# Mixing's SSM half by token block: the first block through both column halves, then the second

## The reference, cut to what matters

```python
merged = jnp.concatenate([rms_norm_2(y_ssm, g_ssm_out[l]), rms_norm_2(y_attn, g_attn_out[l])], axis=-1)
h = h + rms_norm_2(merged @ w_out[l], g_post_mix[l])

hn = rms_norm_2(h, g_pre_ffn[l])
gu = hn @ w_gate_up[l]
ff = (jax.nn.silu(gu[..., :D_FF]) * gu[..., D_FF:]) @ w_down[l]
h = h + rms_norm_2(ff, g_post_ffn[l])
```

## Time and profile before

| | |
|---|---|
| median of 3 runs | 795.18 us (792.7 to 795.67) |
| profiled execution, its own time | 792.62 us |
| its span, first to last instruction | 790.8 us |
| TensorE matmul / weight load busy | 775.9 us (98%) / 678.8 us (86%) |
| VectorE, ScalarE, GpSimd busy | 514.8 (65%), 405.1 (51%), 233.1 (29%) |
| mean granted TensorE clock | 0.998 |

### The profile page before, as it was taken

The page is one execution under the profiler, slowest core; times in us unless marked ns, Lnnn a source line. Parts: engine busy times, 40 slices in busy tenths (PEclk is TensorE's granted clock), DMA queues, the critical chain, the costliest instruction groups (busy, mean ns, idle before and its releaser), DMA issues.

```text
span 790.8 us, 12710 instructions
## 1 busy us (share of the span) xinstructions
PE 775.9 (98%) x5139; PEld 678.8 (86%) x5139; DVE 514.8 (65%) x753; ACT 405.1 (51%) x649; POOL 233.1 (29%) x186
## 2 busy tenths in 40 slices
PE   8999999999999999999999999998999999999996
PEld 7889988999889889987778888997887888888885
DVE  4746874764557557865557965776678676777453
ACT  5744446534465535344335545717766555556341
POOL 3031895670742000046009910126002111011010
PEclk9999999999999999999999999999999999999999
DMA  9897995387621554654545555430363656655641
GB/s 231 201 247 210 239 229 129 90 195 172 158 80 55 188 184 134 213 179 142 158 134 159 185 192 183 136 132 2 133 225 117 195 184 214 186 184 164 223 175 54
DMA packets 78110, 130.72 MB, mean 165 GB/s; under 512 B 4447, under 2 KB 28243, under 8 KB 77923
## 3 DMA queue, kind: packets, MB, share of 16 engines
q1 hardware_dynamic: 76608, 124.96, 54.2%
q0 software_dynamic: 1200, 4.83, 1.9%
q10 hardware_dynamic: 242, 0.11, 0.0%
HBM read 128.82 MB, written 1.06 MB: 164 GB/s over the span
## 4 chain that ended last, share of the span: by engine, by line
PE 87%; DVE 4%; DMA 3%; ACT 3%; issue 1%; POOL 0%; DVEq 0%; SPq 0%; POOLq 0%; ACTq 0%
PE ps L1515 13%; PE ps L1519 13%; PE ps L1523 13%; PE ps L1555 10%; PE ps L1534 6%; PE ps L1538 6%; PE ps L1542 6%; PE ps L1559 5%; DMA stage<-in_even_w_in 3%; PE ps L1626 2%; PE ps L1645 2%; DVE w_lo L921 1%; ACT w_hi L634 1%; PE ps L1658 1%; PE ps L1657 1%
## 5 line engine op out<-in xcount | busy, mean ns | idle before, releaser
L921 DVE TENSOR_TENSOR w_lo<-stage,w_hi 128x1024 fp32r<-128x1024 f32 x226 | 297.6, 1337 | 162.7 <-ACT w_hi L634 162.0
L634 ACT ACTIVATE w_hi<-stage 128x1024 fp32r<-128x1024 f32 x232 | 242.2, 1060 | 236.9 <-PE ps L1523 112.3
L1515 PE MATMUL ps<-w_hi,act_t 128*128 128x512 f32 (+1 forms) x376 | 102.7, 395 | 1.5 <-ACT w_hi L634 1.0
L1523 PE MATMUL ps<-w_lo,act_t 128*128 128x512 f32 (+1 forms) x376 | 98.7, 385 | 0.1
L1555 PE MATMUL ps<-act_t,w_hi 128*128 128x512 f32 x352 | 88.3, 393 | 0.7 <-DVE act_t L958 0.7
L1515 PEld LDWEIGHTS ps<-w_hi,act_t 128*128 128x128 f32 x376 | 67.9, 188 | 16.8 <-issue 2.8
L1523 PEld LDWEIGHTS ps<-w_lo,act_t 128*128 128x128 f32 x376 | 69.6, 188 | 14.8 <-DVE w_lo L921 0.6
L1519 PE MATMUL ps<-w_hi,act_t 128*128 128x512 f32 (+1 forms) x312 | 81.6, 384 | 0.0
L1555 PEld LDWEIGHTS ps<-act_t,w_hi 128*128 128x128 f32 x352 | 63.3, 189 | 12.2 <-issue 0.9
L1519 PEld LDWEIGHTS ps<-w_hi,act_t 128*128 128x128 f32 x312 | 57.6, 188 | 12.1 <-issue 0.2
L1534 PE MATMUL ps<-act_t,w_hi 128*128 128x256 f32 x416 | 58.9, 284 | 0.4 <-ACT w_hi L634 0.4
(11 more groups left out here) (364 smaller groups left out, 1197.4 us busy)
## 6 DMA issues: line engine op xcount, KB each, us to landing
stage<-in_even_w_in SPq DMA_DIRECT2D x64, 512.0 KB, 5.5
stage<-in_odd_w_in SPq DMA_DIRECT2D x48, 512.0 KB, 4.1
stage<-in_w_gate_up SPq DMA_DIRECT2D x44, 512.0 KB, 4.5
stage<-in_w_down SPq DMA_DIRECT2D x22, 512.0 KB, 4.4
stage<-in_even_w_out SPq DMA_DIRECT2D x16, 512.0 KB, 4.2
stage<-in_odd_w_out SPq DMA_DIRECT2D x16, 512.0 KB, 3.9
stage<-in_w_in SPq DMA_DIRECT2D x10, 512.0 KB, 3.7
stage<-in_w_out SPq DMA_DIRECT2D x8, 512.0 KB, 5.0
```

The costliest lines, as they stand in the source:

```text
L634: nc.scalar.activation(w_hi[:, u % RING, :], stage[:, u % RING, :], ACT.Copy).then_inc(hi_ready, 1)
L921: nc.vector.tensor_tensor(w_lo[:, u % RING, :], stage[:, u % RING, :], w_hi[:, u % RING, :].bitcast(F32), ALU.subtract).then_inc(lo_ready, 1)
L1515: mm(out[:, b, :], a_hi(k)[:, tok[b]], hi[:, i, :], start=(k == 0), stop=False)
L1523: ins = mm(out[:, b, :], a_hi(k)[:, tok[b]], lo[:, i, :], start=False, stop=(k == k_tiles - 1))
```

## The change

- TensorE: `mix_ssm` runs block 0 through half 0 and half 1, then block 1 through both, twelve matmuls for each pair. All four weight units are released in block 1. Before the last six matmuls (block 1, half 1, second unit) TensorE turns block 0 of x. Behind them it waits for half 0's drain, issues `keep_busy(9)`, waits for all low parts of block 0 (`first_lo`) and turns block 1.
- The turned tiles are split by block, 128 x 128 each (`hi_of_block`, `lo_of_block`), 16 + 16 instructions for 8 + 8. Block 0's stand ahead of block 1's last sum on VectorE, and ahead of its last square on ScalarE.
- `mix_gain` writes its product to another buffer (`ssm_out` for half 0, `gate_z` for half 1), so it waits for the sum alone and no longer for the square. `x_add` reads there.
- The sums go in the order (0,0), (1,0), (0,1), (1,1).
- `take_attn_half(1)` comes ahead of `squares(5)` on ScalarE.
- The splits of weights stand elsewhere. Up to the last unit of `mix_ssm` they are made before mixing's sums, both parts. The high parts of the next two follow block 0's squares. VectorE makes the low parts of the FFN's units between and behind the low parts of block 1 of x.

```diff
 # ScalarE
             hi_of_turned(3 * KD + 20, 4, 4, COL_GSSM)
+            take_attn_half(1)
             squares(5, lambda b: ssm_out[:, b, :], lambda b: gate_z[:, b, :])
-            take_attn_half(1)
-            ahead(("mix_ssm", 0))
...
+            split_hi(last_unit[("mix_ssm", 1)] + 1)
...
+            def hi_of_block(b, made):
+
+                for k in range(KD):
+                    act.wait_ge(x_turned, KD * b + (k | 1) + 1)
+                    o = 4 * BANK + k * S + b * P
+                    nc.scalar.activation(act_t[:, k, b * P:(b + 1) * P], ps[:, o:o + P], ACT.Copy, scale=col[:, COL_FFN + k:COL_FFN + k + 1]).then_inc(made, 1)
+
+            mix_squares(0, 0)
+            mix_squares(1, 0)
+            split_hi(last_unit[("mix_ssm", 1)] + 3)
+            mix_squares(0, 1)
+            hi_of_block(0, first_hi)
+            mix_squares(1, 1)
+            hi_of_block(1, act_hi)
             ahead(("mix_ssm", 1))
-            hi_of_turned(3 * KD + 24, KD, 0, COL_FFN)
             act.wait_ge(x_ready, 2 * NB)
 # VectorE
+            gained = (ssm_out, gate_z)
+
             def mix_gain(c, b):
 
-                dve.wait_ge(squared, squared_count(5) + 2 * c + b + 1)
-                return TT(mixed[:, b, halves[c]], mixed[:, b, halves[c]], row_a[:, halves[c]], ALU.mult)
+                dve.wait_ge(mixed_ready, 2 * b + c + 1)
+                TT(gained[c][:, b, :], mixed[:, b, halves[c]], row_a[:, halves[c]], ALU.mult).then_inc(drain_sem(("mix_ssm", c)) if b == 1 else mix_gained, 1)
...
+            split_lo(last_unit[("mix_ssm", 1)] + 1)
+            for c in range(2):
+                chunk_drained(dve, ("mix_attn", c))
+                dve.wait_ge(mix_block, c + 1)
+                mix_sum(c, 0)
+                mix_gain(c, 0)
+            mix_mean(0)
+            x_add(0, 0)
+            x_add(1, 0)
             chunk_done(dve, ("mix_ssm", 0))
...
+            mix_sum(0, 1)
+            mix_gain(0, 1)
+            lo_of_block(0, range(KD), first_hi, 0, first_lo)
             chunk_done(dve, ("mix_ssm", 1))
             mix_sum(1, 1)
...
+            mix_gain(1, 1)
             mix_mean(1)
...
             x_add(0, 1)
             x_add(1, 1)
-            lo_of_turned(3 * KD + 24, 4, 0, COL_FFN, KD)
-            split_lo(next_unit[0] + 1)
-            lo_of_turned(3 * KD + 28, 4, 4, COL_FFN + 4, KD + 4)
+            lo_of_block(1, range(4), act_hi, 3 * KD + 24, act_lo)
+            split_lo(last_unit[("mix_ssm", 1)] + 2)
+            lo_of_block(1, range(4, 8), act_hi, 3 * KD + 24, act_lo)
             split_lo(last_unit[("ffn", 0)] + 1)
 # TensorE
+            def turn_block(b):
+
+                for k in range(KD):
                     if k % 4 == 0:
                         pe.wait_ge(x_ready, 2 * b + k // 4 + 1)
                     o = 4 * BANK + k * S + b * P
-                    ins = nc.tensor.transpose(ps[:, o:o + P], x[:, b, k * P:(k + 1) * P], ident[:])
-                    if b == 1:
-                        ins.then_inc(turned, 1)
+                    nc.tensor.transpose(ps[:, o:o + P], x[:, b, k * P:(k + 1) * P], ident[:]).then_inc(x_turned, 1)
...
+                        if b == 1:
+                            ins.then_inc(unit_used, 1)
+                        if (b, c, j) == (1, 1, 0):
+                            turn_block(0)
+                    if b == 0:
+                        ins.then_inc(mix_block, 1)
+            chunk_drained(pe, ("mix_ssm", 0))
+            keep_busy(9, number[("mix_ssm", 0)] % 2 * 2)
+            pe.wait_ge(first_lo, KD)
+            turn_block(1)
```

More of the change, by code:

```diff
@@ L260, in build @@
         turned, act_hi, act_lo = sem("turned"), sem("act_hi"), sem("act_lo")
-        x_ready, h_ready, mix_gained = sem("x_ready"), sem("h_ready"), sem("mix_gained")
+        x_ready, x_turned, h_ready, mix_gained, first_hi, first_lo = (sem(n) for n in ("x_ready", "x_turned", "h_ready", "mix_gained", "first_hi", "first_lo"))
         dve_step, act_step, pool_step = sem("dve_step"), sem("act_step"), sem("pool_step")
@@ L867, in _, with mix_squares @@
             hi_of_turned(3 * KD + 20, 4, 4, COL_GSSM)
+            take_attn_half(1)
             squares(5, lambda b: ssm_out[:, b, :], lambda b: gate_z[:, b, :])
-            take_attn_half(1)
-            ahead(("mix_ssm", 0))
[L871 to L875, removed]
+            split_hi(last_unit[("mix_ssm", 1)] + 1)
+            def mix_squares(c, b):
+                act.wait_ge(mixed_ready, 2 * b + c + 1)
+                half = slice(c * 512, (c + 1) * 512)
+                nc.scalar.activation(junk[:, b, half], mixed[:, b, half], ACT.Square, scale=D**-0.5, accum_out=(sumsq, sumsq_b)[c][:, 12 + b:13 + b]).then_inc(squared, 1)
+            def hi_of_block(b, made):
[10 more added lines that the diff above has]
+            hi_of_block(1, act_hi)
             ahead(("mix_ssm", 1))
-            hi_of_turned(3 * KD + 24, KD, 0, COL_FFN)
             act.wait_ge(x_ready, 2 * NB)
@@ L1358, in mix_sum @@
                 STT(mixed[:, b, halves[c]], result(("mix_ssm", c))[:, b, :], rstd[:, 10 + b:11 + b], mixed[:, b, halves[c]], ALU.mult, ALU.add).then_inc(mixed_ready, 1)
+            gained = (ssm_out, gate_z)
             def mix_gain(c, b):
-                dve.wait_ge(squared, squared_count(5) + 2 * c + b + 1)
-                return TT(mixed[:, b, halves[c]], mixed[:, b, halves[c]], row_a[:, halves[c]], ALU.mult)
+                dve.wait_ge(mixed_ready, 2 * b + c + 1)
+                TT(gained[c][:, b, :], mixed[:, b, halves[c]], row_a[:, halves[c]], ALU.mult).then_inc(drain_sem(("mix_ssm", c)) if b == 1 else mix_gained, 1)
             def mix_mean(b):
-                dve.wait_ge(squared, squared_count(5) + 2 + b + 1)
+                dve.wait_ge(squared, squared_count(5) + 2 * b + 2)
                 c = slice(12 + b, 13 + b)
@@ L1373, in x_add @@
                 dve.wait_ge(rstd_ready, 7 + b)
-                STT(x[:, b, halves[c]], mixed[:, b, halves[c]], rstd[:, 12 + b:13 + b], x[:, b, halves[c]], ALU.mult, ALU.add).then_inc(x_ready, 1)
-            ahead(("mix_ssm", 0))
-            chunk_drained(dve, ("mix_attn", 0))
-            chunk_done(dve, ("mix_ssm", 0))
[L1379 to L1387, removed]
+                if b == 1:
+                    chunk_drained(dve, ("mix_ssm", c))
+                else:
+                    dve.wait_ge(mix_gained, c + 1)
+                STT(x[:, b, halves[c]], gained[c][:, b, :], rstd[:, 12 + b:13 + b], x[:, b, halves[c]], ALU.mult, ALU.add).then_inc(x_ready, 1)
+            def lo_of_block(b, tiles, hi_made, n_hi, made):
+                for k in tiles:
+                    dve.wait_ge(hi_made, n_hi + (k | 1) + 1)
+                    o, tok = 4 * BANK + k * S + b * P, slice(b * P, (b + 1) * P)
+                    STT(act_t[:, KD + k, tok], ps[:, o:o + P], col[:, COL_FFN + k:COL_FFN + k + 1], act_t[:, k, tok].bitcast(F32), ALU.mult, ALU.subtract).then_inc(made, 1)
@@ L1389, in _ @@
             mix_sum(1, 1)
-            chunk_drained(dve, ("mix_ssm", 0))
-            dve.wait_ge(mix_gained, 1)
-            x_add(0, 0)
+            mix_gain(1, 1)
             mix_mean(1)
-            x_add(1, 0)
-            mix_gain(1, 1).then_inc(drain_sem(("mix_ssm", 1)), 1)
-            chunk_drained(dve, ("mix_ssm", 1))
             x_add(0, 1)
             x_add(1, 1)
-            lo_of_turned(3 * KD + 24, 4, 0, COL_FFN, KD)
-            split_lo(next_unit[0] + 1)
-            lo_of_turned(3 * KD + 28, 4, 4, COL_FFN + 4, KD + 4)
+            lo_of_block(1, range(4), act_hi, 3 * KD + 24, act_lo)
@@ L1908, in _ @@
                     o = 4 * BANK + k * S + b * P
-                    ins = nc.tensor.transpose(ps[:, o:o + P], x[:, b, k * P:(k + 1) * P], ident[:])
-                    if b == 1:
-                        ins.then_inc(turned, 1)
+                    nc.tensor.transpose(ps[:, o:o + P], x[:, b, k * P:(k + 1) * P], ident[:]).then_inc(x_turned, 1)
+            hi_there, lo_there = after_lo(3 * KD + 20)
+            for b in range(NB):
+                tok = slice(b * P, (b + 1) * P)
+                for c in range(2):
+                    name = ("mix_ssm", c)
+                    if b == 0:
+                        start_chunk(name)
+                    out = result(name)[:, b, :]
+                    for j in range(2):
+                        hi, lo = unit_of(name, j)
+                        for k in range(2 * j, 2 * j + 2):
+                            hi_there(k)
+                            mm(out, x_hi(4 + k)[:, tok], hi[:, k % 2, :], start=(k == 0), stop=False)
+                        for k in range(2 * j, 2 * j + 2):
+                            lo_there(k)
+                            mm(out, x_lo(4 + k)[:, tok], hi[:, k % 2, :], start=False, stop=False)
+                        lower_there(name, j)
+                        for k in range(2 * j, 2 * j + 2):
+                            ins = mm(out, x_hi(4 + k)[:, tok], lo[:, k % 2, :], start=False, stop=(k == CT - 1))
```

(7 more changed lines are left out.)

## The result

The changed kernel took 799.07 us in the median of 13 runs (796.05 to 801.27), the kernel before beside it 793.97 (13 runs). The ratio is 1.0055, 95% interval [1.0041, 1.0068]: slower by 0.55%, which is 4.4 us (the two medians alone stand 5.1 apart). The forecast of 798.6 stayed within 0.5%, at 0.43%, and the measured ratio is just past it. The profiled execution took 799.87 us, its span 798.1 for 790.8.

What follows compares the result with a forecast made beforehand. The prediction took the chain of waits through TensorE, from mixing to the FFN, as the bound. A late FFN of 2.6 us plus a row stall of 0.8 made 3.4, on the median 795.18 giving 798.6 us; range 796.0 to 801.5.

Steps and rivals of the forecast that it cites:

- Block 0 earlier, mixing later: In mixing: block 0's first x_add comes 3.1 us earlier (593.3 for 596.43), and mixing ends 1.7 us later.
- sum(1,1) behind block 0's low parts: On VectorE: block 1's last sum waits behind block 0's low parts and starts at 598.85 instead of 595.55, 3.3 us late.
- FFN 2.6 us late: On TensorE: the first FFN matmul starts at 603.95 instead of 601.34, with bounds of 2.4 to 3.6 us.
- The chain before: Ahead of the FFN: TensorE waits from block 1's second-half sum through square, mean, power, x_add, transposes and splits, 5.79 us.
- Row stall 0.8: Before FFN chunk 1: later weight loads delay VectorE's row copy and stall TensorE by nothing to 1.0 us, 0.8 taken.
- The clock: Rival, chance 0.25: some 3.5 us idle before block 1's transposes halves TensorE's clock, costing 2 to 2.5 us; total 800.4.
- the forecast's own case: Chance 0.45: the stage loses 3.4 us as summed, giving 798.6 us, a loss just within 0.5%.
- The sum: From mixing to FFN chunk 1: 2.6 us for the late FFN plus 0.8 for the row, 3.4 us.
- Harmless order: Rival, chance 0.10: block 1's last sum starts as its matmuls end, the FFN is only 0.9 us late; 796.1.
- a gain after all: Rival, chance 0.05: block 0's early x removes waits in the FFN's first chunk, at most 1 us; 794.2.
- Queues cost more: Rival, chance 0.15: narrow tiles cost as much as wide ones and the row copy waits in full, 3.5 + 1.0; 799.7.

Runs made afterwards that it cites:

- e3: The changed kernel without block 0's early high and low parts, both blocks split at 128x256 behind block 1's transposes; ratio to the kernel before 1.0016.
- e5: The changed kernel with block 1's last sum, gain and mean ahead of block 0's low parts, its square behind four high parts; ratio to the kernel before 1.0041.
- e4: The kernel before with only the gain's target buffer and wait changed, x_add reading the new buffers; ratio to the kernel before 0.9999.
- e1: The changed kernel with keep_busy(22) for keep_busy(9), 26 more filler records; ratio to the kernel before 1.0048.
- e2: The changed kernel with keep_busy(22) for 9 and the row copied behind two low splits of FFN chunk 1, not three; ratio to the kernel before 1.0020.
- e6: The changed kernel with keep_busy(22) for 9 and the low split of the FFN's first unit ahead of block 0's low parts; ratio to the kernel before 1.0036.
- e8: e5 with the row copied behind two low splits of FFN chunk 1 instead of three; ratio to the kernel before 1.0020.
- e7: The changed kernel with keep_busy(13) for keep_busy(9); ratio to the kernel before 1.0041.

## Why the prediction was right, and where not

- **Block 0 earlier, mixing later.** Held: x_add(0,0) 3.2 us earlier (3.1 predicted), mixing through at + 12.69 (12.74).
- **sum(1,1) behind block 0's low parts.** Held, and shown by e3 and e5: 3.11 us late (3.3), and it starts as soon as its matmuls are done once nothing stands ahead of it. Narrow tiles took 0.26 each (eight high parts in 2.16, eight low parts in 2.16, some 0.26 apart), the value taken.
- **FFN 2.6 us late.** 2.18 measured. Of the 0.43 too much, 0.19 is the sum, which started at + 14.80 for 14.99, and 0.27 the stretch from block 1's mean to x_add(0,1), for which the middle between powers of 0.57 and 0.99 us was taken: it took 0.83, and both powers took 0.56 to 0.57. The 0.03 beyond 0.43 go the other way.

```profile
603.95 0.56 POOL L604 TENSOR_TENSOR rstd<-sumsq,neg_half 128x1 f32<-128x1 f32 x1 [7.26 <-DVE sumsq L1386]
```

- **The chain before was not quite the one named.** There x_add(0,1) followed gain(1,1) on VectorE directly, 0.2 us after the power had ended (598.32), and that gain stood behind x_add(1,0). So the profile's chain runs through the sum, square and gain of (1,0) and not through sum(1,1), which is why the gain's new buffer alone brings 0.50 (e4). From sum(1,1) to the FFN it took 5.79 before, 5.15 in e3 and 4.86 in the changed kernel, where the prediction has 5.10.

```profile
597.83 0.68 DVE L1363 TENSOR_TENSOR mixed<-mixed,row_a 128x512 f32<-128x512 f32 x1
```

- **Row stall 0.8.** The mechanism held (e1, e2, e6), the size was 1.6, past the bound of 1.0. M+10's high split starts at 616.17 in e1, 10.7 us after the FFN's start, where the latest landing I took stands at 10.2. Its load was issued when predicted (5.09 us behind the FFN's start for 5.05) but took 5.6 us, and I had taken 5.1 as the upper bound, although go to 6.2; with 6.2 the bound on the stall would have been 2.1. The reason given, that closely spaced loads hold each other up, fits but is not shown: in the changed kernel, e1, e2 and e6 the load of M+8, with none close ahead of it, took 3.4 to 3.5, and that of M+10, issued 1.1 us behind M+9's, took 5.1 to 5.6. No run changes the spacing alone.
- **The clock.** Here the forecast's own case failed. A chance of 0.25 was given to the fall, and it occurred. Each of the 13 runs shows a mean clock of 0.992 to 0.997, and a fall of 3.4 us takes 0.002 off the mean. Of 35 runs of the kernel before, 27 show 0.998 or more, of the 12 of e1 8 and of the 12 of e2 11. So I take it that the fall occurred in all 13; the profile shows it in one. Four other kernels whose profiles show no fall in this stage (e3, e4, e5, e8) have 5 or 6 of 10 or 12 runs at 0.997 or less, so a single such mean proves nothing; thirteen of thirteen speak for it. Its price was put at 2.3 and 0.3 for the transposes. It was 1.6 and nothing, as the clock fell behind the transposes, and as predicted it swallowed the row stall.
- **The sum.** The stage costs 3.76 us: 2.18 + 1.57 for the clock. The forecast said 2.6 + 0.8 = 3.4. The total is near for partly the wrong reason: a start too late by 0.4, and a row stall in the place of the clock's. With either one of the two 1.6 the time is the same, which is why e1 gained nothing in its stage. The absolute time was luck in part: the forecast of 798.6 stands on the median of three runs, 795.18, and the thirteen runs beside the changed kernel have 793.97. On that base it would have been 797.4, for 799.07 measured.
- **The rivals.** "Harmless order" and "a gain after all" fell: sum(1,1) waited for the low parts (+ 14.80), and no longer in e3 and e5. "Queues cost more" fell on its narrow tiles; the row was as late as it said and later, but behind the clock. Where the 2.18 come from: 0.57 remain when block 0's early parts are left out (e3), although the gain's new buffer gives back 0.50 (e4). So TensorE's order by blocks costs about 1.1 and block 0's early parts 1.6; of the latter, 1.26 go by moving them behind the sum (e5). The 1.1 is a difference between kernels, not a run of its own.

Open: whether the wait and fall of the clock around 520 us is more frequent in the changed kernel. 8 of its 13 runs are at 0.995 or less, where two falls would put them, and 4 of the 35 of the kernel before. If so, it is a part of the 4.4 us over the stage's 3.76. The profiles show that the wait is not the changed kernel's own: it is there in seven of ten (e8 0.68, e4 and e7 0.96, e1 1.58, the changed kernel 1.78, e6 2.32, e2 2.33), e4 with the old order among them, and not in the kernel before, e3 and e5. The clock fell behind the three longest. How often it comes in each kernel no run tells.

## What to carry to other kernels

Work that is made ready early belongs behind the chain that ends last, on every engine's queue: block 0's parts were off the path until they stood ahead of block 1's sum. When a split or a copy is moved, follow what its slot releases; here a load three steps on became the next wait. And if removing a cost moves nothing, look for a second one of the same length that lay under it.

## What the runs showed of the hardware

- The clock fell after 2.29 us (e7) and 3.20 us (after) without TensorE work, each time after work had begun again, and stayed at 1.2 GHz for some 3.4 us (1.03 and 1.57 us of the first unit's time). Around 520 us it fell likewise behind waits of 1.78, 2.32 and 2.33 us (after, e6, e2), and not behind 1.58 (e1). 1.21 us (e3) and 1.49 us (e5) in this stage brought no fall in their profiles either. The Trainium skill ("TensorE: Matmul & The Clock Gate", Part 1, the clock gate) has idling halve the clock, and these runs agree.
- GpSimd's power of 128x1 took 0.55 to 0.57 us while VectorE idled, 0.57 (before) and 0.55 (e5) beside a sum and low parts of VectorE with one input in PSUM, and 0.99 beside an x_add and a gain, whose inputs both lie in SBUF; e4 repeats this (0.57 and 1.00). In the changed order nothing of VectorE's ran beside block 1's power, so the 0.57 was the value to take. A tensor_scalar of 128x2 took 0.19 us while VectorE idled (e6, 612.68) and 0.99 and 2.36 beside low splits of weights (after, 611.17; before, 605.02). The Trainium skill ("SBUF — State Buffer", SBUF: two separate sides) has a VectorE instruction with two inputs in SBUF and a GpSimd instruction that reads SBUF exclude each other at a shared port pair. x_add is such an instruction, and the rows agree; no run here tests it.
